# Last expert's rows kept on chip and added by 0/1 products; the other rows loaded into freed weight buffers

## The reference

```python
    aff = jax.nn.sigmoid(x2.astype(f32) @ router_w.astype(f32))
    ...
    w_sel = jnp.take_along_axis(aff, idx, axis=-1)
    gate = w_sel / jnp.sum(w_sel, axis=-1, keepdims=True)
    ...
    def expert_block(args):
        xblk, e = args
        h = jax.nn.silu(xblk @ w_gate[e]) * (xblk @ w_up[e])
        return h @ w_down[e]
    ...
    y = jnp.zeros((N, D), x.dtype).at[tok_sorted].add(yb[dest] * gate_sorted[:, None].astype(x.dtype))
    ...
        x = layer_norm(DEEPNORM_ALPHA * x + ffn, ln2_g[l], ln2_b[l])
```

## Time and profile before

| | us |
|---|---|
| median of 3 runs | 2147.21 (2146.64 to 2147.99) |
| the profiled execution, its own time | 2145.4 |
| its span, first to last instruction | 2143.6 |

### The profile page before, as it was taken

The page is one execution under the profiler, slowest core; times in us unless marked ns, Lnnn a source line. Parts: engine busy times, 40 slices in busy tenths (PEclk is TensorE's granted clock), DMA queues, the critical chain, the costliest instruction groups (busy, mean ns, idle before and its releaser), DMA issues. The chain is left out here.

```text
span 2143.6 us, 36559 instructions
## 1 busy us (share of the span) xinstructions
PE 2062.6 (96%) x14742; PEld 1673.5 (78%) x14743; DVE 1269.0 (59%) x1291; ACT 925.2 (43%) x1069; POOL 514.2 (24%) x377
## 2 busy tenths in 40 slices
PE   8998999999999999999999999999899999999996
PEld 6777777767787887888887788788688888888882
DVE  4767422234410565356478723356788888888885
ACT  4672122242101553022246421001677777777763
POOL 4232311112340102233323332201122222222100
PEclk9999999999999999999999999999899999999998
DMA  4445544424431544321143422231799999999986
GB/s 151 134 123 195 181 118 124 128 99 161 160 132 37 128 109 154 113 69 40 50 133 119 175 86 99 101 118 59 265 406 389 389 382 388 385 381 386 384 332 240
DMA packets 138137, 408.48 MB, mean 191 GB/s; under 512 B 38736, under 2 KB 60112, under 8 KB 112800
## 3 DMA queue, kind: packets, MB, share of 16 engines
q1 hardware_dynamic: 123104, 367.40, 48.8%
q10 hardware_dynamic: 5552, 22.02, 2.7%
q0 software_dynamic: 9360, 17.32, 2.2%
HBM read 353.53 MB, written 69.93 MB: 198 GB/s over the span
## 5 line engine op out<-in xcount | busy, mean ns | idle before, releaser
L3612 DVE TENSOR_TENSOR ex_sb_low<-landed,high 128x2048 fp32r<-128x2048 f32 x192 | 431.0, 2286 | 61.4 <-ACT high L3541 57.9
L3541 ACT CAST high<-landed 128x2048 fp32r<-128x2048 f32 x186 | 346.2, 1912 | 38.4 <-PE ex_ps_u L169 35.5
L3426 POOL DMA_INDIRECT y_rows<-ex_sb_y,slot_row x32 | 32.2, 1006 | 438.7 <-ACT ex_sb_y L3556 414.5
L167 PE MATMUL ex_ps_g<-high,ex_sb_xt 128*128 128x512 f32 x260 | 104.9, 403 | 2.4 <-DVE ex_sb_xt L3606 2.4
L169 PE MATMUL ex_ps_g<-high,ex_sb_xt 128*128 128x512 f32 x260 | 102.1, 393 | 0.0
L168 PE MATMUL ex_ps_g<-ex_sb_low,ex_sb_xt 128*128 128x512 f32 x260 | 102.0, 392 | 0.0
L167 PE MATMUL ex_ps_u<-high,ex_sb_xt 128*128 128x512 f32 x260 | 101.4, 390 | 0.5 <-DVE ex_sb_low L3612 0.5
L169 PE MATMUL ex_ps_u<-high,ex_sb_xt 128*128 128x512 f32 x260 | 101.2, 389 | 0.0
L168 PE MATMUL ex_ps_u<-ex_sb_low,ex_sb_xt 128*128 128x512 f32 x260 | 101.2, 389 | 0.0
L169 PE MATMUL ex_ps_y<-high,ex_sb_ht 128*128 128x512 f32 x248 | 96.8, 390 | 0.0
L167 PE MATMUL ex_ps_y<-high,ex_sb_ht 128*128 128x512 f32 x248 | 96.6, 390 | 0.0
(11 more groups left out here) (704 smaller groups left out, 5575.2 us busy)
## 6 DMA issues: line engine op xcount, KB each, us to landing
landed<-exp_up SPq DMA_DIRECT2D x64, 1024.0 KB, 8.3
landed<-exp_gate SPq DMA_DIRECT2D x64, 1024.0 KB, 7.7
landed<-exp_down SPq DMA_DIRECT2D x62, 1024.0 KB, 8.5
chunk_ch<-slab SPq DMA_DIRECT2D x4, 2048.0 KB, 7.5
merged_d<-room SPq DMA_DIRECT2D x16, 512.0 KB, 2.9
landed<-ssm_c SPq DMA_DIRECT2D x16, 512.0 KB, 4.8
cb_sb_y<-y_rows SPq DMA_DIRECT2D x16, 512.0 KB, 9.5
si_sb_w<-w_tiles SPq DMA_DIRECT2D x14, 512.0 KB, 3.6
```

Source lines behind the costliest of these rows:

```text
L167: nc.tensor.matmul(out, lhs[0], rhs[0], start=start, stop=False)
L3426: pool.indirect_dma_start(k.y_rows, bass.IndirectOffsetOnAxis(ap=k.slot_row[:, e:e + 1], axis=0), y[e % 2][:, :], None, bounds_check=2 * T ...
L3541: nc.scalar.copy(part_half(high[part], h), part_half(k.landed[part], h)).then_inc(high_ready[part], 1)
L3612: nc.vector.tensor_tensor(part_half(low[part], half), part_half(k.landed[part], half), part_half(high[part], half), ALU.subtract).then_inc ...
```

## The change

1. `scatter(31)` is gone. Expert 31's result is multiplied by the share of each of its rows while it is copied out of PSUM: ACT writes the rounded product to `last_y[0]`, DVE the rest to `last_y[1]`, each in two halves. The shares are fetched by row: POOL writes `gates` to HBM (`share_d`, two DMAs of 1024 elements of 4 bytes) and gathers 128 of them into `share` before `scatter(28)`.
2. `combine` adds these rows by two more products for each half: a 0/1 matrix `at_token` (slot by token, built by DVE at the end of `experts`) times `last_y[0]` and `last_y[1]`, in float32r.
3. The rows of `y_rows` that expert 31 no longer writes are set to zero by one scatter of `nought` after expert 4's gather.
4. SP issues the 16 row loads at the end of `experts`, once the scatters up to expert 30 have landed, into the memory of `high` and `low` of parts 1 and 2. The buffers `low0..2` move from the stage to the trunk for this.
5. DVE's share work moves ahead of `body(E - 3)` and `body(E - 2)`, its overflow chain, three instructions longer, ahead of `times_up(E - 1)`.
6. In `overflow_experts`, PE does three idle products (`IDLE_AHEAD`) when there is no overflow. The 12 of `combine` are gone.
7. In `combine`, the PSUM tile has four buffers, the scaled row goes to a buffer `g` of its own, so that `scale(t)` stands before `norm(t - 1)` and doesn't wait for the square; ACT takes a root of `eps` first; the last tile is joined, normed and stored in halves.

```diff
+def load_rows(eng, k, t, landed):
+    for n, y in enumerate(rows_of(k, t)):
+        eng.dma_start(y, k.y_rows[n * T + t * P:n * T + (t + 1) * P, :]).then_inc(landed, 16)
...
                     sp.dma_start(k.landed[LAST_DOWN][:, n * D:(n + 1) * D], row.partition_broadcast(P)).then_inc(k.x1_in[2], 16)
+                for b in range(2):
+                    sp.wait_ge(y_out[b], ROWS_OUT[b])
+                sp.wait_ge(rows_cleared, 16)
+                for part, read in ((1, E + 1), (2, E)):
+                    sp.wait_ge(used[part], read)
+                    for t in range((part - 1) * NT // 2, part * NT // 2):
+                        load_rows(sp, k, t, k.y_in[t])
...
+                    if e == 4:
+                        pool.wait_ge(cleared, 2)
+                        pool.indirect_dma_start(k.y_rows, bass.IndirectOffsetOnAxis(ap=k.slot_row[:, E - 1:E], axis=0), nought, None,
+                                                bounds_check=2 * T - 1, oob_is_err=False).then_inc(rows_cleared, 16)
+                pool.wait_ge(shared, 2)
+                for n in range(2):
+                    pool.dma_start(k.share_d[n * T:(n + 1) * T].rearrange("(t p) a -> p (t a)", p=P), k.gates[:, :, n],
+                                   allow_slow_non_contiguous=True).then_inc(share_out, 16)
+                pool.wait_ge(share_out, 32)
+                pool.indirect_dma_start(share[:, :], None, k.share_d, bass.IndirectOffsetOnAxis(ap=k.slot_row[:, E - 1:E], axis=0),
+                                        bounds_check=2 * T - 1, oob_is_err=False).then_inc(share_in, 16)
-                for e in range(E - 4, E):
+                for e in range(E - 4, E - 1):
                     scatter(e)
+                for b in range(2):
+                    pool.wait_ge(y_out[b], ROWS_OUT[b])
...
-                nc.scalar.copy(y[1][:, HALF:D], ps_u[:, :]).then_inc(last_kept, 1)
+                act.wait_ge(share_in, 16)
+                for half, ps in enumerate((ps_g, ps_u)):
+                    act.wait_ge(last_done, half + 1)
+                    nc.scalar.activation(k.last_y[0][:, half * HALF:(half + 1) * HALF], ps[:, :], ACT.Copy, scale=share[:, :]
+                                         ).then_inc(last_high, 1)
...
-                nc.vector.tensor_copy(y[1][:, 0:HALF], ps_g[:, :]).then_inc(last_kept, 1)
+                over(nc.vector.tensor_copy(kept_token[:, :], k.slot_token[:, E - 1:E]))
+                over(nc.vector.tensor_tensor_scan(iota[:, :], mat(k, "ones"), mat(k, "ones"), -1.0, ALU.mult, ALU.add))
+                over(nc.vector.tensor_tensor(from_tile[:, :], kept_token[:, :].to_broadcast([P, NT]), mat(k, "slot0", NT), ALU.subtract))
+                times_up(E - 1)
+                low_w(E, 1, LAST_DOWN)
...
+                nc.vector.tensor_tensor(k.at_token[:, :].rearrange("p (t a) -> p t a", a=P), iota[:, :].unsqueeze(1).to_broadcast(
+                    [P, NT, P]), from_tile[:, :].unsqueeze(2).to_broadcast([P, NT, P]), ALU.is_equal).then_inc(listed, 1)
...
+                    nc.vector.scalar_tensor_tensor(k.last_y[1][:, at], ps[:, :], share[:, :], k.last_y[0][:, at], ALU.mult, ALU.subtract
+                                                   ).then_inc(last_kept, 1)
...
+                def idle():
+                    for n in range(IDLE_AHEAD):
+                        mm(ps_y[:, n % 2, :], k.high[0][:, 0:P], k.high[0][:, 0:HALF], start=True, stop=True)
...
-                for n in range(IDLE_PRODUCTS):
-                    nc.tensor.matmul(ps[1][:, 1, :], k.high[n % 3][:, 0:P], k.high[n % 3][:, 0:HALF], start=True, stop=True)
...
                     for half in range(2):
...
+                        out = ps[t % TILES_AHEAD][:, half, :]
+                        for n, y in enumerate(rows_of(k, t)):
+                            nc.tensor.matmul(out, diag[t % 2][n][:, :], y[:, ends[half]], start=(n == 0), stop=False)
+                        for n in range(2):
+                            m = nc.tensor.matmul(out, at_token[:, t, :], k.last_y[n][:, ends[half]], start=False, stop=(n == 1))
+                        m.then_inc((half_weighted, weighted)[half], 1)
...
+                nc.scalar.activation(warm[:, :], eps[:, :], ACT.Sqrt).then_inc(table_in, 1)
...
+                join_halves(0, 0)
+                scale(0)
+                for t in range(1, LAST):
+                    join(t)
+                    scale(t)
+                    norm(t - 1)
+                join_halves(LAST, 1)
+                scale(LAST)
+                norm(LAST - 1)
+                b = LAST % 2
+                invert(LAST)
+                for half in range(2):
+                    v.scalar_tensor_tensor(res[b][:, ends[half]], g[b][:, ends[half]], sd[b][:, :], ln[:, 1, ends[half]],
+                                           ALU.mult, ALU.add).then_inc((half_normed, normed)[half], 1)
```

188 lines of the change are left out of this document (105 added, 83 removed).

## The result

The changed kernel takes 2161.24 us (median of 4 runs, 2161.19 to 2164.69), the kernel before beside it 2147.6: a ratio of 1.007 with a 95% interval of 1.0056 to 1.0083. That is 13.6 us slower, where 5.8 were forecast. The time lay inside the range of 2147.5 to 2162, but the forecast's mechanism is less than half of it. The profiled execution took 2161.22 us with a span of 2159.4.

The account below looks back on a forecast made before the run. PE was taken to bound the expert stage, then a start at 2100.4 and a DVE-paced pipeline of 39.6 us. DVE's last result 6.1 us later, less 0.3 for the store, gave 2147.2 + 5.8 = 2153.0, range 2147.5 to 2162.

Parts of the forecast that it names:

- Start of the row loads: End of the expert stage: SP's loads wait only for scatter(30), landing in 3.4 us, and start 5.9 us earlier.
- the term for the shares: POOL ahead of scatter(28): the two share transfers take 5.4 us, within 10 us of room, so no delay.
- SP's queue ahead of the barrier: End of the experts: 16 issues take SP 8.26 us while all engines wait; `combine` starts at 2101.5, formerly 2094.7.
- ACT ahead of the first product: Start of `combine`: table load, root and diagonals take 1.5 + 0.7 us, so PE starts at 2103.8.
- PE as the bound: Pipeline of `combine`: four products for each half make PE need 4.4 us a tile, above DVE's 4.14; 35.2 us for eight.
- The clock: First products of `combine`: PE runs at half speed for 4.2 us of real work, losing 2.1 us.
- The tail: Behind PE's last product: DVE's joins, scaling and results of the last tiles take 5.1 us, ending at 2146.2.
- What is hidden: Expert stage: the zeros' scatter, DVE's share work, the longer overflow chain and `at_token` cost nothing, covered by PE or idle time.
- The first rival: Expert stage: the share transfers hold up POOL and the last product, 6 us late, for 2159; chance 0.25.
- The second rival: End of the experts: SP's issues are short (0.1 us each) and hold no engine, for 2146.5; chance 0.08.
- The third: Start of `combine`: PE's clock is already up, 2.1 us less, for 2150.9; chance 0.17 together with quicker issues.

Follow-up runs that it names:

- e12: The changed kernel run again without any edit, beside the kernel before: 2161.3 us, ratio 1.0076.
- e3: The changed kernel with all 16 row loads issued by SP at the start of `combine`, as before the change: 2156.7 us, ratio 1.0045.
- e4: The changed kernel with only the four loads of tiles 0 and 1 issued ahead of the barrier, the other twelve in `combine`: 2154.7 us, ratio 1.0032.
- e7: The changed kernel without the product of `last_y[1]`, three products for each half in place of four: 2158.9 us, ratio 1.0056.
- e5: The changed kernel with 44 idle products behind the last expert product and six in place of three in the overflow block: 2160.7 us, ratio 1.0072.
- e2: The changed kernel with the shares sent in one transfer of 128 pieces of 64 bytes, seven DVE instructions working out the gather row: 2155.1 us, ratio 1.0039.
- e8: The changed kernel with 128-piece shares, scatter(28) ahead of them, four loads early, ten and six idle products, root table behind the first diagonals: 2145.5 us, ratio 0.9996.
- e10: The kernel of e8 with only tile 0's two loads ahead of the barrier and fewer idle products (four and three): 2145.7 us, ratio 1.0000.
- e11: The changed kernel with the shares in one transfer of 128 pieces and scatter(28) ahead of it in POOL's queue: 2155.7 us, ratio 1.0046.
- e14: The kernel of e8 without its added idle products (three remain) and with the root's table ahead of the diagonals: 2148.5 us, ratio 1.0010.
- e1: The changed kernel with scatter(28) ahead of the share transfers, scatter(29) behind their issue, then the gather and scatter(30); pieces unchanged: 2159.8 us, ratio 1.0052.
- e15: The kernel of e5 run again without any edit, beside the kernel before: 2159.8 us, ratio 1.0059.

## Why the prediction was wrong

By its own steps, changed kernel against forecast:

1. **Start of the row loads: forecast 2089.7, measured 2098.4.** This is the step that failed, 8.7 of the 10.0 us by which the span (2149.4 forecast, 2159.4 measured) is off. Under it lies the term for the shares: the forecast put their two transfers at 5.4 us, which made no delay, and they took 13.8. Of the 8.7 us, 0.6 is a shift ahead of it (0.3 ahead of the stage, 0.3 in it). 4.3 is scatter(30) later by the shares. 3.9 is its landing, 7.25 us in place of the 3.4 that it took in the trace of before. I took the shortest because few loads ran beside it there, but the shares, by way of the late down weights, moved the loads of x1 under it. How much of the loss lies in the issue and how much in the landing differs between executions: in e12, the same kernel, scatter(30) went out 8.3 us later against L than before the change and was waited for 4.3 us, and L to S was 41.0 there and 40.0 here.
2. **SP's queue ahead of the barrier: right.** 8.44 us for the issues (8.26 forecast), and from SP's first issue to combine 12.36 in place of 11.8; of these 0.6 us, 0.4 are the three idle products, 1.65 us at half speed where the forecast had 1.2. e3 and e4 show the issues as the cause.
3. **ACT ahead of the first product: right.** 2.13 us, forecast 2.3. The next instruction of ACT starts 0.01 us behind the table load's end; no draining is to be seen, as the forecast had it from the trace.
4. **PE as the bound, 4.4 us a tile: right.** 4.36, and e7 shows it.
5. **The clock: right in size.** Half speed for 4.9 us behind the first product (4.2 forecast), some 2.4 us lost; e5 has 2.3. In the other traces with half speed it was 3.6 to 6.1 us.
6. **The tail: 5.7 us in place of 5.1.** DVE was still at the result of tile 5 when tile 7's products came.
7. **What is hidden: not quite.** From the first scatter of the stage to L pass 502.53 us before and 502.83 with the change, in e12 too, and the 0.3 is there at the next scatter already (17.61 in place of 17.33 us behind the first): the zeros' scatter stands ahead of a gather, which goes out 4.5 us behind the stage's first scatter in place of 1.3. How this comes to 0.3 us was not followed further. The seven small instructions of DVE in e2, e8, e10, e11 and e14 add 0.47 more (503.30). Neither was free.

**The first rival was the case.** Its mechanism and threshold were right (10 us of room, 13.8 taken: 3.8 us of delay, where PE's waits came to 4.7), its size was not: it had 6 us for POOL's delay and no term for what the pieces do to other transfers. And the choice between its ends was badly argued. The bounds were 5.4 and 24.4 us; I took the lower because 1072 small packets were through in 2.7 us. Those ran at another place with little beside them. The middle of the bounds (14.9) would have been 1.1 from the truth, and beyond the threshold of 10. The trace of before could have told who would be hit, though not how hard: SP's loads of x1 hang on the landing of the last down weights, and these were on the way at the very time of the shares.

**The second rival** (issues hold nobody) fell with e3 and e4. **The third** (the clock is up) is what e5 shows in one trace; it didn't happen in the changed kernel.

**Where the gain went.** The last scatter did leave the path: in e8, 7.4 us pass from the start of the last expert product to the first real one where the kernel before needs 10.7. Of these 3.3 us, 1.3 go into the pipeline (P to D 40.9 in place of 39.6, by four products for each half), and 0.8 into the stage ahead of L.

## What to carry to other kernels

Count the pieces of a transfer, not its bytes: 8 KB in 2048 pieces took longer than a load of 1 MB (13.8 us and 6.7), and they delayed the loads of the down weights that were under way, so look for who waits for such loads. Before loads are issued early, ask which barrier the issuing engine must still reach; issue what the first tile needs and leave the rest behind the barrier. Where a bound decides whether a wait shows at all, the sum should take the side that the load on the queues at that time suggests, or the forecast should be given as two cases.

## What was not expected of the hardware

- 2 x 1024 pieces of 4 bytes from SBUF to HBM, beside 1 MB loads, took 12.3 to 16.5 us until POOL went on. The down weights issued from 2056 to 2066 landed in 10.0 to 14.4 us (median of each trace) in place of 6.7. The same bytes as 128 pieces of 64 took 5.9 us (e2), and the down weights beside them landed in 7.5 to 8.4 (e2, e8, e10, e11, e14). For 2 us of that time the DMA engines, no less busy than without the pieces, moved 99 GB/s in place of 393.
- Scatter(30), 128 rows, landed in 4.3 to 8.4 us in the ten traces with the 2048 pieces: 8.4 us where it went out 8.9 us behind the first load of x1 (e1), 7.25 at 12.6 us behind it (changed), 4.3 at 16.1 us behind it (e12). In the seven other traces, where x1 had landed ahead of it, it took 3.4 to 3.9 us.
- With equal gaps of about 2 us between products the clock fell in one execution and not in the other (e15, e5). It rose 3.6 to 6.1 us behind the first real product.
- The time from the start of the program to the stage of the experts differs by up to 6.8 us between the traces of kernels that are the same up to there. Its cause is open. Below some 2 us only stretches inside a trace told anything here.
